# Expert weights used in plain fp32 as they land, 64 token slots stationary, two pieces side by side in the array

## What is computed

```python
# h: 256 tokens x 1024; 32 experts, each token goes to 4
logits = h @ w_router + b_router
top, idx = top_k(logits, 4); p = softmax(top)
for e in range(32):                 # for the tokens that chose e
    gu = h @ w_gu[e] + b_gu[e]      # 1024 x 2048: gate half, up half
    g, u = min(gate, 7), clip(up, -7, 7)
    y += p_e * (((u + 1) * g * sigmoid(1.702 * g)) @ w_down[e] + b_down[e])
x = x + g2 * y
```

## Time and profile before

| | us |
|---|---|
| median of 3 runs | 3067.77 |
| lowest, highest | 3065.08, 3068.77 |
| span of the profiled execution | 3055.5 |
| run median less span | 12.3 |
| expert stage, first unit to last scatter | 1045.8 to 2112.5 |

### The profile page before, as it was taken

The page is one execution under the profiler, slowest core; times in us unless marked ns, Lnnn a source line. Parts: engine busy times, 40 slices in busy tenths (PEclk is TensorE's granted clock), DMA queues, the critical chain, the costliest instruction groups (busy, mean ns, idle before and its releaser), DMA issues. The chain is left out here.

```text
span 3055.5 us, 43841 instructions
## 1 busy us (share of the span) xinstructions
PE 2865.2 (94%) x17128; PEld 2408.0 (79%) x17129; DVE 2183.8 (71%) x3290; ACT 1644.3 (54%) x2277; POOL 151.9 (5%) x175
## 2 busy tenths in 40 slices
PE   7899999899989899999999999997987999978998
PEld 4799899757779777777777777776965999966998
DVE  3467666566746799999999999997664566574665
ACT  2355545322135478788877887884432445432453
POOL 0232242000000000000000000000000000000000
PEclk8899999999969799999999999998975999985999
DMA  6431110073136799999999999993620456420553
GB/s 197 61 67 29 35 49 1 11 237 101 42 96 181 276 374 381 385 377 379 385 378 381 380 381 378 383 391 121 202 73 1 139 175 181 131 87 0 166 183 121
DMA packets 257977, 604.64 MB, mean 198 GB/s; under 512 B 26114, under 2 KB 82665, under 8 KB 257385
## 3 DMA queue, kind: packets, MB, share of 16 engines
q1 hardware_dynamic: 256684, 601.35, 56.9%
q10 hardware_dynamic: 1085, 0.45, 0.1%
HBM read 596.29 MB, written 5.44 MB: 197 GB/s over the span
## 5 line engine op out<-in xcount | busy, mean ns | idle before, releaser
L2410 DVE TENSOR_TENSOR moe_raw_r<-moe_raw,moe_hi 128x2048 fp32r<-128x2048 f32 x320 | 719.5, 2286 | 7.7 <-ACT moe_hi L2613 7.7
L2613 ACT ACTIVATE moe_hi<-moe_raw 128x2048 fp32r<-128x2048 f32 x320 | 599.8, 1907 | 7.8 <-PE banks L2497 4.4
L2953 PE MATMUL banks<-xs_r,w_hi 128*128 128x272 f32 (+1 forms) x1632 | 474.8, 291 | 28.4 <-DVE w_raw_r L3375 19.7
L2957 PE MATMUL banks<-xs_r,w_raw_r 128*128 128x272 f32 (+1 forms) x1632 | 472.3, 289 | 0.0
L2954 PE MATMUL banks<-xs_r,w_hi 128*128 128x272 f32 (+1 forms) x1632 | 469.7, 288 | 0.0
L3197 ACT ACTIVATE w_hi<-w_raw 128x512 fp32r<-128x512 f32 (+1 forms) x416 | 256.8, 619 | 245.5 <-PE banks L2957 201.5
L2953 PEld LDWEIGHTS banks<-xs_r,w_hi 128*128 128x128 f32 x1632 | 310.9, 190 | 33.5 <-issue 25.5
L2957 PEld LDWEIGHTS banks<-xs_r,w_raw_r 128*128 128x128 f32 x1632 | 310.8, 190 | 2.9
L3375 DVE TENSOR_TENSOR w_raw_r<-w_raw,w_hi 128x512 fp32r<-128x512 f32 (+1 forms) x416 | 271.7, 676 | 56.5 <-ACT w_hi L3197 52.4
L2954 PEld LDWEIGHTS banks<-xs_r,w_hi 128*128 128x128 f32 x1632 | 311.2, 191 | 0.2
L2536 PEld LDWEIGHTS banks<-con,gu_tok 128*128 128x128 f32 x1024 | 191.0, 192 | 29.1 <-ACT gu_tok L2625 9.6
(11 more groups left out here) (506 smaller groups left out, 5775.9 us busy)
## 6 DMA issues: line engine op xcount, KB each, us to landing
moe_raw<-in_w_gu SPq DMA_DIRECT2D x256, 1024.0 KB, 8.2
moe_raw<-in_w_down SPq DMA_DIRECT2D x128, 1024.0 KB, 10.1
w_raw<-in_w_ff SPq DMA_DIRECT2D x256, 256.0 KB, 3.0
w_raw<-in_w_in SPq DMA_DIRECT2D x112, 256.0 KB, 2.7
gdn_w<-in_w_in SPq DMA_DIRECT2D x32, 512.0 KB, 4.0
mod_ring<-in_w_mod SPq DMA_DIRECT2D x16, 1024.0 KB, 5.4
ring_mod<-in_w_mod SPq DMA_DIRECT2D x4, 2048.0 KB, 20.1
wh<-in_w_in SPq DMA_DIRECT2D x8, 1024.0 KB, 9.5
```

Source lines behind the costliest of these rows:

```text
L2410: dve.tensor_tensor(rest[n % UNITS][:, :], raw[n % UNITS][:, :], hi[n % HI_SLOTS][:, :].bitcast(F32), ALU.subtract).then_inc(los, 1)
L2613: act.activation(hi[n % HI_SLOTS][:, :], raw[n % UNITS][:, :], ACT.Copy).then_inc(his, 1)
L2953: pe.matmul(bank, w_hi, x[:, 0, 0:n_cols], start=first, stop=False)
L2957: ins = pe.matmul(bank, w_lo, x[:, 0, 0:n_cols], start=False, stop=last)
```

## The change

Weights stay as they land and are used in plain fp32 by PE; `moe_hi`, `rounded`, `lo`, `x_kept` and the split of the tokens go. The stationary operand of a matmul is 64 token slots (128 x 64), and the two 128-row pieces of a unit write to partitions 0 to 63 and 64 to 127 of the same bank, so they take the left and the right half of the array's columns; the fold in `turn` adds the two, as it did the high and low parts. The ring grows from 12 units to 16; the last two lie in memory that the routing uses, so SP waits for its end before loading them. The matmuls of turn, slots, fetch and scatter are no longer interleaved with those of units. `fetch` gathers from one plain fp32 copy of the tokens, with eight matmuls in place of 16. Core of the diff:

```diff
-UNITS, HI_SLOTS, OVER_HI = 12, 6, 4
+UNITS, OVER_UNITS, LATE_UNITS = 16, 12, 2
...
-        xs_own = sb("moe_xs", [P, 2, KT, 2 * SLOTS], FR)
-        xs_lent = xT_r[:, :, :].rearrange("p k t -> p (k t)").rearrange("p (j k n) -> p j k n", j=2, k=KT)
+        xs = sb("moe_xs", [P, 2, 2, KT, SLOTS])
...
                 def act_second(e, h):
                     dve.wait_ge(sig, 2 * e + h + 1)
                     dve.wait_ge(clip, 2 * e + h + 1)
-                    dve.scalar_tensor_tensor(g[:, 0], g[:, 1], 1.0, sg[:, :, :], ALU.add, ALU.mult).then_inc(prod, 1)
-                    dve.wait_ge(prod, 2 * e + h + 1)
-                    dve.tensor_copy(acs[:, 4 * h:4 * h + 4, 0:SLOTS], g[:, 0]).then_inc(act_hi, 1)
-                    dve.wait_ge(act_hi, 2 * e + h + 1)
-                    dve.tensor_tensor(acs[:, 4 * h:4 * h + 4, SLOTS:], g[:, 0],
-                                      acs[:, 4 * h:4 * h + 4, 0:SLOTS].bitcast(F32), ALU.subtract).then_inc(act_ready, 1)
+                    dve.scalar_tensor_tensor(acs[:, 4 * h:4 * h + 4, :], g[:, 1], 1.0, sg[:, :, :], ALU.add, ALU.mult)\
+                       .then_inc(act_ready, 1)
...
                 for n in range(3):
                     load_unit(sp, n)
                 sp.dma_start(bd, a["b_down"][0]).then_inc(bd_in, 16)
-                sp.dma_start(kept, xT[:, :, :]).then_inc(x_kept, 16)
-                for n in range(3, UNITS):
+                for n in range(3, UNITS - LATE_UNITS):
+                    load_unit(sp, n)
+                sp.wait_ge(on_dve, marks["end"])
+                for n in range(UNITS - LATE_UNITS, UNITS):
                     load_unit(sp, n)
...
-                def unit(ph, e, q, beside=None):
+                def unit(ph, e, q):
                     n = place[ph, e, q]
-                    x = (acs if ph == "d" else xs_of(e))[:, 2 * q:2 * q + 2, :]
-                    pe.wait_ge(los, n + 1)
+                    x = acs if ph == "d" else xs_of(e)
+                    pe.wait_ge(loaded[n % UNITS], n // UNITS * 16 + 16)
+                    for c in range(2):
+                        for k in range(2):
+                            ins = pe.matmul(ps[pair(e) + c][k * SLOTS:(k + 1) * SLOTS, :], x[:, 2 * q + k, :],
+                                            raw[n % UNITS][:, k * D + c * 512:k * D + c * 512 + 512], start=(q == 0), stop=(q == 3))
+                    ins.then_inc(used, 1)
+
+                def fetch_part(r, bank):
                     for i in range(8):
-                        k, w, c = i // 4, (hi[n % HI_SLOTS], rest[n % UNITS])[i // 2 % 2], i % 2
-                        ins = pe.matmul(ps[pair(e) + c][:, :], x[:, k, :], w[:, k * D + c * 512:k * D + c * 512 + 512],
-                                        start=(q == 0 and i < 2), stop=(q == 3 and i > 5))
-                        if i == 7:
-                            ins.then_inc(used, 1)
-                        if beside is not None:
-                            beside(i)
...
+                        m, t = i // 2, i % 2
+                        k = 4 * (r % 2) + m
+                        ins = pe.matmul(ps[bank][:, m * P:(m + 1) * P], htok[:, t, k * P:(k + 1) * P],
+                                        pick[:, r // 2 % 2, t, :, 0:SLOTS], start=(t == 0), stop=(t == 1))
+                    return ins
...
                     if nxt:
+                        pe.wait_ge(s_out, e + 1)
                         if e + 2 < NEXP:
                             pe.wait_ge(x_out, e + 2)
-                        else:
-                            pe.wait_ge(s_out, e + 1)
                         unit("g", e + 1, 0)
-                        unit("g", e + 1, 1, lambda i: turn(e, 0, i))
-                        unit("g", e + 1, 2, lambda i: turn(e, 1, i))
+                        turn(e, 0)
+                        unit("g", e + 1, 1)
+                        turn(e, 1)
+                        unit("g", e + 1, 2)
                         unit("g", e + 1, 3)
...
                         unit("u", e + 1, 0)
-                        unit("u", e + 1, 1, lambda i: slots_then_fetch(e + 1, i))
-                        scatter(e, (lambda i: fetch(e + 2, 4 + i)) if far else None)
-                        unit("u", e + 1, 2, (lambda i: fetch(e + 2, 8 + i)) if far else None)
+                        unit("u", e + 1, 1)
+                        slots_in(e + 1)
+                        scatter(e)
+                        if e + 3 < NEXP:
+                            fetch(e + 2)
+                        unit("u", e + 1, 2)
                         unit("u", e + 1, 3)
```

More of the change, by code:

```diff
@@ L2467, in _ @@
-                dve.wait_ge(x_kept, 32)
+                    if e % 2 and e + 4 < NEXP:
+                        dve.wait_ge(slots, e + 1)
+                        hot_of(e + 3)
+                        hot_of(e + 4)
+                    for h in range(2):
+                        act_first(e, h)
+                        act_second(e, h)
                 last_dve(dve)
@@ L2532, in turn @@
-                def turn(e, h, i):
-                    s, m = i // 4, i % 4
-                    if i == 0:
-                        pe.wait_ge(gu_out, 2 * e + 2)
-                    ins = pe.matmul(ps[pair(e) + h][:, i * SLOTS:(i + 1) * SLOTS], gs[:, s, (4 * h + m) * P:(4 * h + m + 1) * P],
-                                    fold, start=True, stop=True)
-                    if i == 7:
-                        ins.then_inc(turned, 1)
-                def scatter(e, beside=None):
+                    x = acs if ph == "d" else xs_of(e)
@@ new lines, in fetch, with slots_in, turn @@
+                def fetch(n):
+                    r = n + 1
+                    pe.wait_ge(hot, r // 2 * 2 + 2)
+                    if n >= 2:
+                        pe.wait_ge(y_out, n - 1)
+                    fetch_part(r, pair(n) + 1).then_inc(gath, 1)
+                def slots_in(e):
+                    if e:
+                        pe.wait_ge(y_out, e)
+                    slots_of(pe, hot_at(e), lambda t: gate[:, t, e:e + 1], pair(e + 1)).then_inc(slots, 1)
+                def turn(e, h):
+                    pe.wait_ge(gu_out, 2 * e + 2)
+                    for i in range(8):
+                        s, m = i // 4, i % 4
+                        ins = pe.matmul(ps[pair(e) + h][:, i * SLOTS:(i + 1) * SLOTS], gs[:, s, (4 * h + m) * P:(4 * h + m + 1) * P],
+                                        fold, start=True, stop=True)
+                    ins.then_inc(turned, 1)
@@ L2588, in _ @@
                         for h in range(2):
-                            for i in range(8):
-                                turn(e, h, i)
+                            turn(e, h)
                     pe.wait_ge(t_free, 2 * e + 2)
```

248 lines of the change are left out of this document (57 added, 191 removed).

## The result

| | before | after |
|---|---|---|
| median of 4 runs each, us | 3067.94 | 2979.9 |
| lowest, highest | 3065.08, 3068.77 | 2974.59, 2991.11 |
| span of the profiled execution | 3055.5 | 2972.8 |

The ratio is 0.9726, with an interval of 0.9703 to 0.9748: 88 us faster. Taken twice more, on two chips and each time beside runs of before, the ratio was 0.9739 [0.9702, 0.9775] and 0.9745 [0.9726, 0.9763].

A forecast was written before the change was run, and what follows sets the result against it. PE was taken as the bound, DVE close behind. 33.1 - 31.4 = 1.7 us over 31 experts is 53, plus 2 for the ends: 55 off the 3055.5 span gives 3000.5, plus 12.3 is 3013 us; range 2985 to 3170.

The forecast's parts named there:

- 31.4 us an expert: PE time of one expert after the change: units 20.6, turn 3.7, gather 1.8, slots 0.7, scatter 3.4, shape changes 1.2.
- Change of shape: PE switching between unit matmuls and the others: six an expert at 0.2 us, 1.2 us, bounds none to 1.8.
- My own range: Range of the likeliest case: 2985 us, with 30.6 us an expert, up to 3045 with 1 us an expert more.
- Routing itself keeps its length: Routing ahead of the experts: same matmuls, as many gather records as before, so no change in time.
- the ends: First units, at half clock as now, and last expert up to its scatter: 2 us off for both.
- 12.3 above the span: Run time taken as 12.3 us over the profiled span, turning a span of 3000.5 into 3013 us.
- The series: Rival for the units: the two pieces don't run together, 52 us an expert, 3670 us; chance 0.15.
- rows 7: Trace of before, line 3001: plain fp32 row pieces, read as four at once with 32 rows, two with 64.
- The bare loads: Rival: pieces run together but weight loads aren't hidden, 36.2 us an expert, 3164 us; 0.15 including anything else between.
- The DMA rival: Rival for the expert stage: DMA stays the bound at 381 GB/s, 33.0 us an expert, 3063 us; chance 0.08.
- SP's new wait for the end of routing: Before loads 14 and 15: met about when SP arrives; 5 us late would be covered by 14 units of backlog.

The follow-up runs named there:

- e5_half_loads: After, loading only one piece of each weight unit from the second round of the ring on, PE work unchanged: 2974.77 us, 30.94 us an expert.
- e3_one_half: After with both pieces of a unit written to the left half of the array, one after the other: 3649.14 us, 51.52 us an expert.
- e9_before_plain_gather: Before with the 32 matmuls of the first gather, ahead of the bias matmuls, in plain fp32: 3063.79 us, ratio 0.9985.
- e1_turns_together: After with the second g unit moved behind both turns, two changes of shape fewer an expert: 2978.72 us, ratio 0.9719.
- e7_one_break: After with slots, gather, scatter and both turns in one run, two changes of shape an expert in place of six: 2967.99 us, ratio 0.9679.
- e10_one_break_ring12: e7_one_break with the ring cut from 16 to 12 units: 2979.37 us, ratio 0.9723.
- e4_halves_apart: After, issuing both column ranges of one piece of a unit and then both of the other: 2978.36 us, 31.05 us an expert.
- e8_turns_between: After with each turn cut in two around the column ranges of its g unit, four more changes of shape: 3001.8 us, ratio 0.9785.

## Why the prediction was wrong

The direction, the mechanism and the bound were right: PE sets the pace after the change (e5_half_loads), pieces in the two halves run together (e3_one_half), loads are hidden, the DMA follows. That PE set the pace before too rests on the view of waits; no run tests it. The miss is 33 us, and it is in sizes. Between the first two profiles the span fell by 82.7 us, and the parts are: 3.8 the stage was reached earlier, 7.1 to the first unit, 4.4 to the first turn, 63.5 for 29 steps, 4.1 for the last two steps, 0.5 to the last scatter, -0.6 behind it (82.8 by rounding).

**The term "31.4 us an expert" was 0.46 too large.** Its parts against what after shows: units 20.6, as forecast. Turns: 32 records at 0.1115 are 3.57, forecast 3.7, as I had taken the 0.115 of the first run in the earlier trace rows and not the 0.108 of the second. Slots 0.64 for 0.7. Gather 1.78 for 1.8. Scatter 3.43. Change of shape 6 x 0.15 = 0.9, forecast 1.2: the 0.2 of the earlier trace rows is of another pair of shapes, with pieces in rows. The sum is 30.9; the step is 30.94. Over 31 steps the forecast took 53 us off and the trace shows 67.6, so 14.6 of the miss lie here. My own range went down to 30.6 for the step, so this term alone would have left the time inside the range, at about 2998. What put it outside is the next two terms and the early arrival.

**The step "Routing itself keeps its length" failed.** It became 7.1 us shorter between the two profiles (2.9 to 7.9 over all pairs of before and after in the table). The same eight bias matmuls took 3.6 at full clock where they had taken 7.1 at half, and the gather, with as many records as before, 3.8 where it had taken 7.0. Why the clock stood higher is only made likely by e9_before_plain_gather. The forecast named the clock only as something that might fall. The row was there: the bias matmuls of the earlier trace rows at clock 0.50, the same eight records that cost half of that at full clock. I had read it as a rate and not as something that the change could move. Together with the first units, of which about 2.3 is the half clock under the first unit of before and 1.2 are 8 units at 1.717 instead of 1.87 (worked out from the granted clock and the rates, not shown by a run), the ends gave 11.5 and not 2.

**"12.3 above the span" was not a constant.** After's median lies 7.1 above its profiled span; 5.2 of the miss. And 3.8 is the earlier arrival in the first profile of after, which is chance: the arrival varies over 15 us among the profiles with the same code ahead of it. 14.6 + 9.5 + 3.8 + 5.2 = 33.1.

**Rivals.** The series was priced at 3670 and measured at 3649 when forced, with a step of 51.5 for 52: rows 7 were the right row to decide by. The bare loads didn't appear; the rule of the Trainium skill, page "TensorE: Matmul & The Clock Gate", section "Part 3: Packing small matmuls", that a weight load overlaps a running matmul only when its row group differs, would have given 36.2 a step by the forecast's price. The trace disagrees: the loads of 0.14 us lie under matmuls of the same rows in after and in e3_one_half. The same section of the Trainium skill also lets a load into a background weight buffer go ahead of running matmuls, which the forecast didn't take up; the traces fit that, and no run here shows whether it is the reason. The DMA rival fell with 409 GB/s throughout, and e5_half_loads shows that the bytes could be halved. It was close all the same: 12 units at 2.576 are 30.9 us, hardly less than the step of 30.94. e1_turns_together, with 30.65, already asks faster than that, and its smallest lead falls from 16 to 8 us; e7_one_break uses all of it up. Before moved only 381 GB/s, which is what a step of 33.1 asks for: 12.58 MB in 33.1 us is 380. By its records most of its units too landed 2.56 us after the one before; the average is 2.76, as gaps of up to 5 us come where few are on their way: 2.8 and 2.9 on average with two and three, 2.6 with four, where after has seven. e6_before_half_loads, before with half the loads, was to test this rival for before and gave no result, so it stays argued there.

**Waits.** SP's new wait for the end of routing cost nothing to be seen, and the ring of 16 brought nothing in after itself. I had given the ring no price, which was right, for a reason that I had not seen: its worth is in the reserve when the DMA is the slower one, 7 us in e10_one_break_ring12.

## What to carry to other kernels

When several engines prepare data only to make a matmul cheaper, cost the matmul in its plain form in two halves of the array first: two half-width plain fp32 streams cost here a little less than one full-width split stream did (1.72 us a unit for 1.87), with nothing to prepare. Then group what is left by shape, since each run of one shape pays 0.15 us, and stop when the transfer that follows becomes the bound; from there a deeper ring is worth its bytes, and before that nothing. Of the ends of a stage, price each stretch at half clock as something that a change can move, and of one profiled span, say how far such spans scatter before taking "median less span" for a constant.

## What the runs showed of the hardware

- Two plain fp32 matmuls of 64 stationary columns in the two halves, both reading all 128 partitions, run wholly at once: 0.429 us for a pair of records of 512 columns (after), 0.858 in one half (e3_one_half).
- They still pair when the kernel issues two matmuls of the same half in a row (e4_halves_apart, 0.11 us an expert).
- The loads of 128 x 64 for them, 0.14 us each, lie wholly under matmuls of the same rows, and in e3_one_half of the same half too.
- A change between 128 x 64 and 128 x 128 stationary shapes costs 0.145 to 0.147 us (e1_turns_together, e8_turns_between).
- Loads of 1.0486 MB land every 2.56 us where seven are on their way, with one gap of 3.7 to 4.1 us about every 76 units, 195 us, in after, e7_one_break and e10_one_break_ring12; the average is 2.576 (407 GB/s). The DMA share reads 1.01 at 381 GB/s, 1.03 at 409, and 0.63 at 204.
- The clock in the routing and in the first units differs between profiles of the same kernel, in stretches at half clock of 3.4 to 31 us; e7_one_break had one of 7 us at half clock in its first turns, and after had none there.
